# Attention turn: one piece of products per step, scores beside values, values three steps behind, and the queries' last row at the turn's end

## The reference, cut to what matters

```python
z = jnp.einsum('bhtd,bhsd->bhts', qb, k) * SB_SCALE
mask = (kpos[None, :] < qpos[:, None])[None, None]
log_keep = jnp.where(mask, jax.nn.log_sigmoid(-z), 0.0)
after = lax.cumsum(log_keep, axis=3, reverse=True) - log_keep
w = jnp.where(mask, jnp.exp(jax.nn.log_sigmoid(z) + after), 0.0)
return jnp.einsum('bhts,bhsd->bhtd', w, v)
```

## Time and profile before

| what | value |
|---|---|
| median of 3 runs | 2846.87 us (2843.28 to 2847.82) |
| the profiled execution | 2847.93 us, of which the span from first to last instruction is 2845.5 us |
| PE busy | 2695.4 us, 95% of the span |
| DVE, ACT, POOL busy | 1523.5, 852.6, 364.6 us |
| granted TensorE clock, mean | 0.969 of full speed |

### The profile page before, as it was taken

The page is one execution under the profiler, slowest core; times in us unless marked ns, Lnnn a source line. Parts: engine busy times, 40 slices in busy tenths (PEclk is TensorE's granted clock), DMA queues, the critical chain, the costliest instruction groups (busy, mean ns, idle before and its releaser), DMA issues. The chain is left out here.

```text
span 2845.5 us, 48346 instructions
## 1 busy us (share of the span) xinstructions
PE 2695.4 (95%) x17236; PEld 2534.0 (89%) x17236; DVE 1523.5 (54%) x2579; ACT 852.6 (30%) x1566; POOL 364.6 (13%) x327
## 2 busy tenths in 40 slices
PE   6999999999978999998989999999999999999797
PEld 6888888888758999997979999899999999999697
DVE  4565655565654757575663343444444444444645
ACT  4443434333332434343341112211111111111533
POOL 0232322232331111110110002100000000000300
PEclk8999999999998999999989999999999999999799
DMA  5444344465422242434445433411111111111012
GB/s 138 94 85 87 91 96 90 84 98 81 102 59 38 32 95 32 94 32 67 54 148 178 145 127 96 153 38 45 44 37 44 44 37 44 44 37 44 28 37 92
DMA packets 331856, 214.34 MB, mean 75 GB/s; under 512 B 117828, under 2 KB 312216, under 8 KB 331672
## 3 DMA queue, kind: packets, MB, share of 16 engines
q1 hardware_dynamic: 331672, 211.98, 32.3%
HBM read 164.51 MB, written 47.41 MB: 74 GB/s over the span
## 5 line engine op out<-in xcount | busy, mean ns | idle before, releaser
L136 ACT ACTIVATE w_hi<-w_raw 128x1024 fp32r<-128x1024 f32 x171 | 180.6, 1057 | 812.6 <-PE f_acc L159 448.4
L159 PE MATMUL f_acc<-operand_hi,w_hi 128*128 128x384 f32 x1056 | 353.7, 335 | 0.0
L159 PE MATMUL f_acc<-operand_lo,w_hi 128*128 128x384 f32 x1056 | 353.1, 334 | 0.0
L159 PE MATMUL f_acc<-operand_hi,w_lo 128*128 128x384 f32 x1056 | 352.9, 334 | 0.0
L1048 POOL TENSOR_TENSOR wgt<-wgt,left 128x128 f32<-128x128 f32 (+2 forms) x224 | 227.2, 1026 | 594.2 <-DVE left L1003 367.1
L674 PE MATMUL acc<-operand_hi,w_hi 128*128 128x384 f32 x792 | 289.3, 365 | 5.5 <-PEq L209 5.5
L143 DVE TENSOR_TENSOR w_lo<-w_raw,w_hi 128x1024 fp32r<-128x1024 f32 x171 | 212.1, 1241 | 142.3 <-ACT w_hi L136 141.3
L674 PE MATMUL acc<-operand_hi,w_lo 128*128 128x384 f32 x792 | 268.3, 339 | 0.0
L159 PE MATMUL sacc<-operand_hi,w_hi 128*128 128x384 f32 x768 | 268.2, 349 | 0.0
L674 PE MATMUL acc<-operand_lo,w_hi 128*128 128x384 f32 x792 | 268.0, 338 | 0.0
L1003 DVE TENSOR_TENSOR_SCAN left<-keep,left 128x128 f32<-128x128 f32 (+2 forms) x224 | 220.8, 1011 | 74.6 <-ACT keep L898 72.9
(11 more groups left out here) (335 smaller groups left out, 5333.3 us busy)
## 6 DMA issues: line engine op xcount, KB each, us to landing
w_raw<-in_w_in SPq DMA_DIRECT2D x65, 512.0 KB, 8.7
k_cache<-in_cache_k SPq DMA_DIRECT2D x256, 64.0 KB, 2.0
v_cache<-in_cache_v SPq DMA_DIRECT2D x64, 256.0 KB, 4.7
w_raw<-in_w_gate SPq DMA_DIRECT2D x22, 512.0 KB, 3.7
w_raw<-in_w_up SPq DMA_DIRECT2D x22, 512.0 KB, 3.8
w_raw<-in_w_down SPq DMA_DIRECT2D x22, 512.0 KB, 3.6
s_gate_a<-gate SPq DMA_DIRECT2D x24, 192.0 KB, 1.9
s_o<-o_t SPq DMA_DIRECT2D x8, 576.0 KB, 10.2
```

Of the source, the lines that this page charges most:

```text
L136: act.activation(S.w_hi[u0 % 2][:, :], S.raw[u0 % 2][:, :], ACT.Copy).then_inc(S.hi_done, 1)
L159: last = pe.matmul(acc[:, 0:RBN], w[:, k, :], a[:, k, rows], start=(n == 0), stop=(n == 3 * kts - 1 and more is None))
```

## The change

- The two slots of fill in a step become one (`SLOTS = STEPS`); a turn has 17 steps, not 16.
- Within a step the order on TensorE is now scores, values, fill, rows, transposes, cache, turn_o. It was scores, fill, rows, values, transposes, fill, rows, cache, turn_o.
- Values are taken of double unit `s - 3` (`LAG = 3`), not `s - 2`.
- The second half of the samples moves from the last place of `DU` to the place before the last prompt tile.
- The second four cache turns move from steps 8 to 11 to steps 7 to 10.
- VectorE scans both heads first and then empties banks; SyncE waits for the last read of `o` before it stores a turn's output. `WT = 4` is the old number under a name.

```diff
-        if t == 4:
-            out.append(("s", 0))
-    return out + [("s", 1)]
+        if t in (4, 6):
+            out.append(("s", (t - 4) // 2))
+    return out
...
-STEPS = ND + 2
-SLOTS = 2 * STEPS
+LAG = 3
+STEPS = ND + LAG
+SLOTS = STEPS
...
-CACHE_AT = {1: 0, 2: 1, 3: 2, 4: 3, 8: 4, 9: 5, 10: 6, 11: 7}
-TURN_AT = {S_AT[0] + 3: 0, S_AT[1] + 2: 1}
+CACHE_AT = {1: 0, 2: 1, 3: 2, 4: 3, 7: 4, 8: 5, 9: 6, 10: 7}
+TURN_AT = {d + LAG + 1: j for j, d in enumerate(S_AT)}
...
                     sp.wait_ge(S.tp_drained, t.tp(("o", 1)))
+                    sp.wait_ge(S.o_read, HEAD + NO * (t.i + 1))
...
                         if s < ND:
                             scores(t, s)
-                        fill(t, 2 * s)
-                        rows_of(t, 2 * s)
-                        if 0 <= s - 2 < ND:
-                            values(t, s - 2)
+                        if 0 <= s - LAG < ND:
+                            values(t, s - LAG)
+                        fill(t, s)
+                        rows_of(t, s)
                         if 0 <= s - 1 < ND:
                             transposes(t, s - 1)
-                        fill(t, 2 * s + 1)
-                        rows_of(t, 2 * s + 1)
                         if s in CACHE_AT:
                             cache_t(t, CACHE_AT[s])
...
                         if s < ND:
                             scan(t, 2 * s)
-                        for ev in ROWS_AT[t.last][2 * s]:
+                            scan(t, 2 * s + 1)
+                        for ev in ROWS_AT[t.last][s]:
                             drain(t, ev)
-                        if s < ND:
-                            scan(t, 2 * s + 1)
                         if 0 <= s - 1 < ND:
                             drain(t, ("w", 2 * s - 2))
                             drain(t, ("w", 2 * s - 1))
```

More of the change, by code:

```diff
@@ L404 @@
 NU = len(UNITS)
-STEPS = ND + 2
-SLOTS = 2 * STEPS
+LAG = 3
+STEPS = ND + LAG
+SLOTS = STEPS
 S_AT = [d for d in range(ND) if DU[d][0] == "s"]
 U_OLD = [2 * d + 1 for d in S_AT]
-CACHE_AT = {1: 0, 2: 1, 3: 2, 4: 3, 8: 4, 9: 5, 10: 6, 11: 7}
-TURN_AT = {S_AT[0] + 3: 0, S_AT[1] + 2: 1}
-O_BANKS = [("p", t) for t in range(5)] + [("s", 0)] + [("p", t) for t in range(5, PT)] + [("s", 1)]
+CACHE_AT = {1: 0, 2: 1, 3: 2, 4: 3, 7: 4, 8: 5, 9: 6, 10: 7}
+TURN_AT = {d + LAG + 1: j for j, d in enumerate(S_AT)}
+O_BANKS = [("p", t) for t in range(5)] + [("s", 0), ("p", 5), ("p", 6), ("s", 1), ("p", 7)]
 NO = len(O_BANKS)
@@ L452, in block_steps @@
     for m in range(6 if last else 12):
-        out[block_slot(last, m) // 2].append(m)
+        out[block_slot(last, m)].append(m)
     return out
@@ L474, in tp_events @@
     for s in range(STEPS):
-        ev += ROWS_AT[last][2 * s]
+        ev += ROWS_AT[last][s]
         if 0 <= s - 1 < ND:
             ev += [("w", 2 * s - 2), ("w", 2 * s - 1)]
-        ev += ROWS_AT[last][2 * s + 1]
         if s in CACHE_AT:
@@ L510, in stage_pairs @@
     assert NTP % 2 == 0 and NO % 2 == 0 and NU % 4 == 0 and N % 2 == 0, (NTP, NO, NU)
+    WT = 4
     with ExitStack() as ctx:
@@ L530, in stage_pairs @@
         left = [sb(f"left{n}", [P, SEQ + 1]) for n in range(2)]
-        w_t = [sb(f"w_t{n}", [P, 4, P]) for n in range(4)]
+        w_t = [sb(f"w_t{n}", [P, 4, P]) for n in range(WT)]
         kc = sb("k_cache", [P, 4, 4, 2, HD])
@@ L646, in _ @@
                             cache_v(t, 0)
-                        for ev in ROWS_AT[t.last][2 * s] + ROWS_AT[t.last][2 * s + 1]:
+                        for ev in ROWS_AT[t.last][s]:
                             store_rows(t.i + 1, KV.index(ev), t.tp(ev))
@@ L759, in values @@
                     o = ob[o_bank(d) % 2]
-                    w0, w1 = w_t[u % 4], w_t[u % 4 + 1]
+                    w0, w1 = w_t[u % WT], w_t[u % WT + 1]
                     if DU[d][0] == "p":
@@ L926, in _ @@
                             sigmoids(t, 2 * s + 1)
-                        if 0 <= s - 2 < ND and (DU[s - 2][0] == "s" or DU[s - 2][5]):
-                            read_o(t, s - 2)
+                        if 0 <= s - LAG < ND and (DU[s - LAG][0] == "s" or DU[s - LAG][5]):
+                            read_o(t, s - LAG)
                         for m in BLOCKS_AT[t.last][s]:
@@ L973, in drain @@
                     elif kind == "w":
-                        dve.wait_ge(S.av_done, t.unit(x) - 4)
+                        dve.wait_ge(S.av_done, t.unit(x) - WT)
                         c = UNITS[x][4] // P
-                        dve.tensor_copy(w_t[x % 4][:, 0:c, :], src[:, 0:c * P].rearrange("p (c m) -> p c m", c=c))\
+                        dve.tensor_copy(w_t[x % WT][:, 0:c, :], src[:, 0:c * P].rearrange("p (c m) -> p c m", c=c))\
                            .then_inc(S.tp_drained, 1)
@@ L1026, in _ @@
                             drain(t, ("w", 2 * s - 1))
-                        for ev in ROWS_AT[t.last][2 * s + 1]:
-                            drain(t, ev)
                         if s in CACHE_AT:
```

## The result

The changed kernel takes 2919.15 us (median of 4 runs, 2913.11 to 2923.03) against 2847.35 us for the kernel before in the same session: a ratio of 1.0251, 95% interval 1.0229 to 1.0273. The forecast was 2904 us, slower with a chance of 0.86, and a range of 2876 to 2932. The profiled execution is the fastest of the four (2913.11 us).

The account below looks back on a forecast made before the run. TensorE was taken to bound the attention turns. Stalls of 9.9 us less savings of 1.1 and 1.2 gave 53 us over seven full turns, plus 3.4 in the last: 57 us on 2847.9, so 2904 us, range 2876 to 2932.

Parts of the forecast that it names:

- the rival "much slower": Queue held up by a 512 KB weight load (14 us) and lower clock (12 us): 2930 us, chance 0.10.
- The last turn: Half the fill, no blocks' rows: bank waits 6.5 us, loads 3; with joints +3.4 us, about 76 us long.
- The `tp` banks: Up to four uses follow each other, each waiting for VectorE's emptying: 2.5 + 2.8 + 0.4 us a turn outside steps 5 to 7.
- The cache turn behind the weights: Steps 1, 4, 8, 10: waits for the first head's bank, about 0.6 us each, 2.5 us a full turn.
- a block's rows stand ahead of the weights: Steps 2, 3, 9: second head waits for the block's bank, then cache turn again by 0.2 to 0.25: 2.8 us.
- The loads: Steps 5 to 7: 16 loads of cached keys queue behind key block 2's stores, 4.2 us of stall a full turn.
- R + 16.8: When the loads of cached keys land, R being the turn of key block 2's rows at the end of step 5.
- The clock: Part of the much slower rival: waits of 1.5 to 3 us every turn bring half speed, 12 us for seven turns.
- The joints: Switches between whole-array and half-array products: fewer per step, saving 0.18 us without diagonal mask, 1.1 us a turn.
- The joint from scores to values: New joint where scores and values are neighbours, taken at 0.15 us, bounds nothing and 0.35; 11 times a turn.
- The rival "faster": Banks emptied as fast as filled and loads in time, so only savings remain: 2826 us, chance 0.09.
- old `kv_out` wait: Where a value block was turned behind a late scan: wait goes from there, saving 1.2 us a full turn, 9 us.

Follow-up runs that it names:

- the fill over 16 steps: Changed kernel with its fill spread over the first 16 of 17 steps, so key block 2's rows are turned in step 4: 2877.19 us, ratio 1.0109.
- weights first: Weights' transposes put ahead of the fill within a step; as the only edit to the changed kernel, 2888.79 us, ratio 1.0151.
- Values behind the fill: Against the changed kernel with loads ahead of stores, weights' transposes ahead of the fill and LAG 2 (2833.42 us), values moved behind the fill: 2839.6 us.
- The kernel with 16 filled steps and weights first: Changed kernel with fill over the first 16 of 17 steps and weights' transposes ahead of the fill, loads behind the stores: 2826.06 us, ratio 0.9934.
- the sample last: Changed kernel with weights' transposes ahead of the fill, LAG 2, old sample place, second four cache turns in steps 8 to 11: 2823.52 us, ratio 0.9925.
- with `kv_out` late: Changed kernel with the 16 loads of cached keys issued ahead of key block 2's stores in step 5: 2924.9 us, ratio 1.0280.
- the kernel with both edits: Changed kernel with loads of cached keys ahead of key block 2's stores and weights' transposes ahead of the fill: 2864.27 us; with LAG 2, 2833.42.

## Why the prediction was right, and where its sizes were off

**What bounds it.** Right: TensorE bounds the turns, and its waits, its joints and the clock that went with the waits moved the time.

**The size.** The range held, but in part because errors cancelled. The turns grew by 73.5 us in the profile where 57 were forecast: the loads came later than summed (17 us) and the clock fell (up to 14), both of which I had put into the rival "much slower", while the bank waits were summed too large (some 9). The rest of the kernel then ran 7 us shorter in that execution, which no term of mine foresaw. The last turn is as forecast: 76.6 us, where I had 76.

**The `tp` banks.** Right, and the larger half. The pair of kernels that differ in this alone, the fill over 16 steps with and without weights first, puts it at 51 us. By idle rows it is 38 us less 3, and the 66 waits that went add about 0.2 each from start to start (some 13 us, an estimate by the prediction's reading of the earlier trace rows, 1.2 us for the 1.00 listed); the rest is in part the lower clock (17 us of it against 10) and was not separated. My sum had 2.5 + 2.8 + 0.4 a turn outside steps 5 to 7 and 2.85 inside them, 60 us for seven turns. Two terms were too large. The cache turn behind the weights was taken at 1.54 us and measured 1.39, so each such stall was 0.15 too large. And where a block's rows stand ahead of the weights I added a second wait of 0.2 to 0.25 for the cache turn; the trace has none:

```profile
416.05 0.44 PE L755 MATMUL tp<-ident,wgt 128*128 128x128 f32 x2 [0.55 <-DVE kv_out L959]
416.38 0.66 PE L711 MATMUL tp<-ident,k_cache 128*128 128x128 f32 x4
```

The same holds at 423.30 and 468.79: while TensorE waits for the block's bank and turns the second head, VectorE ends the first head's copy too (415.91 to 416.33). With four cache turns of the first kind in a turn that is 0.6 + 0.7 = 1.3 us a turn, 9 us in all.

**The loads.** Right in kind, and here a size was off: R + 16.8 measured R + 19.2 in the mean of seven turns, which is 17 us in all. I took the stores of sample rows at the 3.84 us of one row of one turn; in the seven turns they took 3.8 to 6.4, and the trace of before had 3.8 to 7.2. The 16 loads took 8.8 to 10.1 us to issue, the longer times where the stores had been short. Whether the 512 KB load of weights ahead of them, which the rival named, holds the stores up was not tested. The cause is narrower than I wrote: not that the loads are late, but that key block 2's stores, 16 loads and value block 0's stores share one queue in three steps. Key block 2 came into step 5 through the rounding of 12 blocks over 17 slots; over 16 of them it costs some 40 us less, clock included.

**The clock.** I put it into a rival (0.10), as a lower clock in every turn. It happened: 41 us at half speed against 7, of which up to 14 us are lost. So both halves of that rival came about, its 14 us of a slower queue as 17 and its 12 us of clock as up to 14, and the time still stayed near the forecast and not at its 2930, by the errors named above.

**The joints.** Right. The joint from scores to values, which no row of before showed, is as taken. A piece with no mask ahead of values, with the fill behind:

```profile
488.80 0.39 PE L725 MATMUL z<-k_lo,q_hi 64*128 64x512 f32 x2
489.12 1.09 PE L769 MATMUL o<-w_t,v_rows 128*64 128x128 f32 x16
490.14 0.44 PE L676 MATMUL acc<-operand_hi,w_hi 128*128 128x384 f32 x1
490.42 0.34 PE L676 MATMUL acc<-operand_lo,w_hi 128*128 128x384 f32 x1
```

Values start 0.89 us after the piece's first scores (488.23), as the fill did in the earlier trace rows, and the first fill product behind the values takes 0.28. Values behind the fill cost 6 us where 8 x 1.1 = 9 were forecast. The Trainium skill (TensorEngine Tiling (Array Packing), Key Properties) says that a change of mode drains TensorE; the trace agrees, with the 0.28 against 0.17 us between fill products.

**The rival "faster".** It gave 2826 us if joints and the old `kv_out` wait were all that counts. The kernel with 16 filled steps and weights first measured 2826.06: the gain that the change holds is real and was hidden under its two new waits. That the two figures agree to a tenth is chance: in its profile the turns are 17.6 us shorter (739.30 against 756.90), not 22, and the rest of the kernel is 6 us shorter.

**Free edits.** LAG 3: right, free by itself (2826.06 with it). The turn's end: the sample last did at least as well (2823.52), so no gain of the new place was shown; these two kernels also differ in LAG and in the steps of the cache turns, so how much is the place alone is open.

## What to carry to other kernels

When work between two uses of a double buffer is moved away, price the latency of the buffer's emptying, not the other engine's load: VectorE was busy 56% of a turn and still cost TensorE some 0.5 to 1 us at most pairs. When a count of steps changes, list again which step each block's end, stores and loads fall into; a rounding put two bursts on one in-order queue and cost some 40 us. Read a transfer's time in every turn of a loop, not in one: 3.84 us was the best of seven. And when a late transfer is put first and the time stays, ask who now waits for what it overtook.

## What the runs showed that I had not expected

- Half clock goes with a wait of TensorE, whatever the wait is for: in each full turn the clock stood at 0.50 for 3.4 to 10.2 us at waits of 2.07 us and more, with the loads late (41 us in all) as with `kv_out` late (44 us, waits up to 10.2), and 58 us with waits up to 8.3. The length of the wait alone does not tell: 2.56 us at 868.5 in the last turn of the changed kernel brought none (clock 1.00 in the window above), nor did one of 3.1 us at 224.7 in the kernel with both edits.
- 16 loads of 64 KB take 8.8 to 10.1 us to issue behind the stores, and 10.1 to 18.3 directly behind a load of 512 KB.
- The kernel with both edits was 31 us faster with LAG 2 in place of 3. The slot count explains it as far as the runs go: with LAG 3 and the fill over 16 steps no cost of LAG was left. The same kernel with LAG 3 and 16 filled steps was not run.
